# Spreading a recurrent branch over two projections, and two outputs of the next projection between a head's steps

## What is computed

```
q, k, v, o, gi, gf, xb, gate = _split(hn @ w_in, ...)      # 1024 -> 6 x 1024 and 2 x 4
h_a = sigmoid(o) * mlstm(q, k, v, gi, gf)                  # 4 heads of 256
h_a = h_a * rsqrt(mean(h_a * h_a) + EPS) * mlstm_norm
xc = causal_conv4(xb) + conv_b                             # the recurrent branch
r = sigmoid(xc @ w_r + b_r); i = sigmoid(xc @ w_i + b_i)   # 8 blocks of 128
log_a = -8 * r * softplus(-lam); a = exp(log_a)
u = sqrt(-expm1(2 * log_a)) * (i * xc)
h_b = scan(h = a * h + u) * gelu(gate)
h = h + concatenate([h_a, h_b]) @ w_out                    # 2048 -> 1024
```

## Time and profile before

| | |
|---|---|
| median of 3 runs | 2597.84 us (2596.29 to 2609.27) |
| profiled execution | 2598.1 us, its span 2596.3 us |
| mean granted PE clock | 0.972 of full speed |
| busy share of the span | PE 95%, DVE 68%, ACT 52%, POOL 0% |

### The profile page before, as it was taken

One profiled execution on the slowest core, in us unless ns is written; L12 is line 12 of the kernel. 1 busy time (PEld: TensorE's weight loads), 2 busy tenths in 40 slices (PEclk: granted clock), 3 DMA queues, 4 the chain that ended last, 5 costly groups with the idle time before them and its releaser, 6 DMA issues.

```text
span 2596.3 us, 54007 instructions
## 1 busy us (share of the span) xinstructions
PE 2457.7 (95%) x18747; PEld 2341.4 (90%) x18747; DVE 1758.2 (68%) x3497; ACT 1348.3 (52%) x2827; POOL 10.3 (0%) x17
## 2 busy tenths in 40 slices
PE   7999998979999999999999999998998999988998
PEld 7899998979989999899988999988877999877998
DVE  6566666977657677776575576656776775777764
ACT  4555556556554444465555565555663444454443
POOL 0000000000000000000000000000000000000000
PEclk9999999999999999899999999999998999998999
DMA  6535563225644333356645356643433555322553
GB/s 203 175 122 170 184 197 117 93 89 171 203 144 130 124 126 121 104 165 185 202 131 181 124 168 192 205 152 121 130 106 98 169 175 174 122 97 90 171 177 129
DMA packets 103383, 385.43 MB, mean 148 GB/s; under 512 B 11344, under 2 KB 13392, under 8 KB 103024
## 3 DMA queue, kind: packets, MB, share of 16 engines
q1 hardware_dynamic: 102784, 381.90, 46.0%
q0 software_dynamic: 496, 2.24, 0.2%
HBM read 383.05 MB, written 1.05 MB: 148 GB/s over the span
## 4 chain that ended last, share of the span: by engine, by line
PE 85%; DVE 9%; ACT 3%; issue 2%; DMA 0%; DVEq 0%; ACTq 0%; SPq 0%
PE acc L488 24%; PE acc L489 23%; PE acc L490 23%; PE acc L667 2%; DVE weights_lo L1628 2%; PE acc L651 1%; PE acc L653 1%; PE acc L652 1%; PE acc L531 1%; PE acc L746 1%; PE acc L705 1%; ACT weights_hi L1062 1%; PE acc L592 1%; PE acc L835 1%; PE acc L726 1%
## 5 line engine op out<-in xcount | busy, mean ns | idle before, releaser
L1628 DVE TENSOR_TENSOR weights_lo<-weights,weights_hi 128x512 fp32r<-128x512 f32 (+1 forms) x1392 | 905.1, 683 | 445.9 <-ACT weights_hi L1062 441.1
L488 PE MATMUL acc<-xn_parts,weights_hi 128*128 128x256 f32 (+1 forms) x3456 | 996.3, 288 | 41.4 <-DVE xn_parts L1742 14.1
L489 PE MATMUL acc<-xn_parts,weights_hi 128*128 128x256 f32 (+1 forms) x3456 | 980.3, 284 | 0.0
L490 PE MATMUL acc<-xn_parts,weights_lo 128*128 128x256 f32 (+1 forms) x3456 | 980.0, 284 | 0.0
L1062 ACT ACTIVATE weights_hi<-weights 128x512 fp32r<-128x512 f32 (+1 forms) x1392 | 811.1, 620 | 250.5 <-PE acc L490 220.6
L488 PEld LDWEIGHTS acc<-xn_parts,weights_hi 128*128 128x128 f32 x3456 | 658.3, 190 | 59.9 <-issue 46.2
L489 PEld LDWEIGHTS acc<-xn_parts,weights_hi 128*128 128x128 f32 x3456 | 657.6, 190 | 1.0
L490 PEld LDWEIGHTS acc<-xn_parts,weights_lo 128*128 128x128 f32 x3456 | 658.5, 191 | 0.0
L488 PE MATMUL acc<-arena_r,weights_hi 128*128 128x256 f32 (+1 forms) x1792 | 511.6, 285 | 9.8 <-DVE arena_r L2090 4.9
L489 PE MATMUL acc<-arena_r,weights_hi 128*128 128x256 f32 (+1 forms) x1792 | 507.3, 283 | 0.0
L490 PE MATMUL acc<-arena_r,weights_lo 128*128 128x256 f32 (+1 forms) x1792 | 507.3, 283 | 0.0
(11 more groups left out here) (286 smaller groups left out, 2494.0 us busy)
## 6 DMA issues: line engine op xcount, KB each, us to landing
weights<-in_ffn_in SPq DMA_DIRECT2D x176, 512.0 KB, 3.6
weights<-in_ffn_out SPq DMA_DIRECT2D x64, 704.0 KB, 4.1
weights<-in_att_in SPq DMA_DIRECT2D x72, 512.0 KB, 3.5
weights<-in_mlp_in SPq DMA_DIRECT2D x64, 512.0 KB, 3.4
weights<-in_mlp_out SPq DMA_DIRECT2D x64, 512.0 KB, 3.5
weights<-in_ret_qk SPq DMA_DIRECT2D x32, 512.0 KB, 3.5
weights<-in_ret_v SPq DMA_DIRECT2D x32, 512.0 KB, 3.8
weights<-in_ret_g SPq DMA_DIRECT2D x32, 512.0 KB, 3.5
```

The source lines that it names most:

```text
L488: nc.tensor.matmul(acc, hi, src_hi, start=first, stop=False)
L489: nc.tensor.matmul(acc, hi, src_lo, start=False, stop=False)
L490: return nc.tensor.matmul(acc, lo, src_hi, start=False, stop=last)
L1628: nc.vector.tensor_tensor(w_lo[sub % phase.subs][:, 0:n, :], raw[slot][:, j * SUB:j * SUB + n, :], w_hi[sub % phase.subs][:, 0:n, :].bitca ...
```

## The change

1. `mlstm_rows` is cut into three parts, done in the first units of `ab_xb`; the convolutions follow one unit each from the fourth unit of `ab_xb` to the third of `ab_gate`.
2. PE computes the two gate products of chunk m right behind unit m of `ab_gate`, in banks 4 to 7. ACT does the sigmoids, a Square and a Tanh there, and the gelu's Tanh one unit later.
3. In the first head's units ACT does the exponent of a chunk per unit, and logarithm and exponent over half the branch (1088 columns) in place of DVE's reciprocals. Square root, products, scans, output and its split are DVE and ACT operations over 2176 columns (scans over 272) in the turns of the heads before the last.
4. The sigmoid of o is one operation of 544 columns per head behind the head's last unit; the fifth turn goes.
5. The last head's steps stand between the pieces of outputs 0 and 1 of `ab_out` (`part_output`): the branch's tiles first, then those of heads 0 and 1, of head 2, and of head 3. `branch_first` reorders the weight rows for it; size and number of the loads stay. `ab_out` then begins with its third output.

The diff, cut to what the mixer's steps need:

```diff
+                tiles = ((8, 9, 10, 11), (12, 13, 14, 15), (0, 1, 2, 3), (4, 5), (6, 7))
+                def part_output(sub, o, part):
+                    pe.wait_ge(split_ready, after.sub0 + sub + 1)
+                    for k in tiles[part]:
+                        pe.wait_ge(*((A["mixed"], k // 2 + 1) if k < DC else (lru_sem["done"], 1)))
+                        last = product(PS[:, o, 0:S2], w_hi[sub % after.subs][:, k % SUB, :], w_lo[sub % after.subs][:, k % SUB, :],
+                                       (ab_hi[k], ab_lo[k]), k == 8, k == 7)
+                    if part != 3:
+                        last.then_inc(sub_multiplied, 1)
...
+                            pe.wait_ge(lru_sem["gates_ready"], 2 * DC)
...
+                last_head = A_HEADS - 1
+                scores(last_head)
+                turn_v(last_head)
+                pe.wait_ge(out_evacuated, evacuated(phase))
+                part_output(0, 0, 0)
+                mix(last_head)
+                part_output(1, 0, 1)
+                part_output(2, 1, 0)
+                part_output(3, 1, 1)
+                part_output(4, 0, 2)
+                head_sum(last_head)
+                part_output(5, 1, 2)
+                part_output(6, 0, 3)
+                part_output(7, 1, 3)
+                part_output(6, 0, 4)
+                part_output(7, 1, 4)
...
+            def gate_projection(src):
+                phase, L = ph["ab_gate"], lru_sem
                 pe.wait_ge(consts2_loaded, 48)
+                for m in range(phase.units):
+                    pe.wait_ge(out_evacuated, FREE_BANKS + phase.out0 - SLOTS + 1 + m)
+                    multiply(phase, m // phase.body, m % phase.body, PS[:, m % SLOTS, 0:S2], src)
+                    pe.wait_ge(L["conv_ready"], m + 1)
+                    if m >= 2:
+                        pe.wait_ge(L["gates_ready"], 2 * (m - 1))
+                    else:
+                        pe.wait_ge(ab_sem["log_in"], 1)
                     for gate, w in ((0, w_r), (1, w_i)):
+                        last = nc.tensor.matmul(PS[:, 4 + 2 * (m % 2) + gate, 0:S2], w[:, m, :], lru_xc[:, m, :], start=True, stop=True)
                     last.then_inc(L["gates_summed"], 1)
...
+                    dense_outputs(ph["ab_out"], lambda k: (ab_hi[k], ab_lo[k]), S2, lambda k: (ab_sem["mixed"], A_HEADS), 1)
...
+            def gelu(c):
+                act.wait_ge(lru_sem["gelu_in"], c + 1)
+                nc.scalar.activation(gelu_t[:, c, :], sq[:, c % 4, :], ACT.Tanh, scale=math.sqrt(2.0 / math.pi))\
+                    .then_inc(lru_sem["gelu_ready"], 1)
+            def gate_projection():
+                L, phase = lru_sem, ph["ab_gate"]
+                nc.scalar.preload_act_table(ACT.Sigmoid)
+                for m in range(phase.units):
...
+                    wait_unit(phase, m // phase.body, m % phase.body)
+                    nc.scalar.activation(lru_gate[:, m, :], PS[:, m % SLOTS, 0:S2], ACT.Copy).then_inc(out_evacuated, 1)
+                    act.wait_ge(L["gates_summed"], m + 1)
+                    for gate, dst, bias in ((0, lru_a, "lru_b_r"), (1, lru_i, "lru_b_i")):
+                        nc.scalar.activation(dst[:, m, :], PS[:, 4 + 2 * (m % 2) + gate, 0:S2], ACT.Sigmoid, bias=param(bias, m))\
+                            .then_inc(L["gates_ready"], 1)
+                    act.wait_ge(out_evacuated, evacuated(phase, m + 1))
+                    nc.scalar.activation(sq[:, m % 4, :], lru_gate[:, m, :], ACT.Square, scale=math.sqrt(0.044715))\
+                        .then_inc(L["gelu_squared"], 1)
+                    act.wait_ge(L["gates_ready"], 2 * m + 1)
+                    nc.scalar.activation(lru_r[:, m, :], lru_a[:, m, :], ACT.Tanh, scale=lam8_neg[:, m:m + 1]).then_inc(L["tanh_ready"], 1)
+                    if m:
+                        gelu(m - 1)
...
+                def output_gate(hd):
+                    o = proj2[:, 24 + 2 * hd:26 + 2 * hd, :]
+                    nc.scalar.preload_act_table(ACT.Sigmoid)
+                    act.wait_ge(out_evacuated, evacuated(phase, (hd + 1) * phase.body))
+                    nc.scalar.activation(o, o, ACT.Sigmoid).then_inc(A["o_ready"], 1)
+                def decay(c):
+                    nc.scalar.activation(lru_a[:, c, :], lru_a[:, c, :], ACT.Exp, scale=lam8[:, c:c + 1]).then_inc(L["decay_ready"], 1)
+                def logarithm(n):
+                    act.wait_ge(L["tanh_ready"], DC)
+                    act.wait_ge(L["input_ready"], DC)
+                    part = slice(n * half, (n + 1) * half)
+                    nc.scalar.activation(y[:, part, :], lru_r[:, part, :], ACT.Ln, bias=one).then_inc(L["logged"], 1)
+                def inverse(n):
+                    act.wait_ge(L["logged"], n + 1)
+                    part = slice(n * half, (n + 1) * half)
+                    nc.scalar.activation(y[:, part, :], y[:, part, :], ACT.Exp, scale=-1.0).then_inc(L["inverse_ready"], 1)
+                def root():
+                    act.wait_ge(L["root_in"], 1)
+                    nc.scalar.activation(lru_r[:, :, :], lru_r[:, :, :], ACT.Sqrt, scale=2.0).then_inc(L["root_ready"], 1)
...
+                        if n == 0:
+                            if i == 0:
+                                gelu(DC - 1)
+                            if i == 1:
+                                root()
+                            exp_tables()
...
+                            decay(n)
+                            if 1 <= n <= 2:
+                                logarithm(n - 1)
+                            if 3 <= n <= 4:
+                                inverse(n - 3)
+                        wait_unit(phase, i, n)
+                        nc.scalar.activation(proj2[:, 8 * (n // 2) + 2 * i + n % 2, :], PS[:, n % 2, 0:S2], ACT.Copy)\
+                            .then_inc(out_evacuated, 1)
+                        if n == 7:
+                            output_gate(i)
...
+                after, hd = phase.after, A_HEADS - 1
+                exp_tables()
+                split(after, 0, 1)
+                weights(hd)
+                values(hd)
+                split_part(after, 0, 2, 0)
+                denominator(hd)
+                split_part(after, 0, 2, 1)
+                squares(hd)
+                split(after, 0, 3)
+                factor(hd)
...
+            def lru_input(c):
+                L = lru_sem
+                dve.wait_ge(L["gates_ready"], 2 * c + 2)
+                nc.vector.tensor_tensor(lru_i[:, c, :], lru_i[:, c, :], lru_xc[:, c, :], ALU.mult).then_inc(L["input_ready"], 1)
+                dve.wait_ge(L["gelu_squared"], c + 1)
+                stt(sq[:, c % 4, :], sq[:, c % 4, :], 1.0, lru_gate[:, c, :], ALU.add, ALU.mult).then_inc(L["gelu_in"], 1)
+            def gate_projection():
+                phase = ph["ab_gate"]
+                for m in range(phase.units):
...
+                    if m < 3:
+                        lru_conv(m + 5)
+                    if m:
+                        lru_input(m - 1)
...
+                        if i == 0:
+                            if n == 0:
+                                lru_input(DC - 1)
+                            if n == 2:
+                                lru_gelu()
...
+                            if n == 7:
+                                lru_root_in()
...
+                        if i == 1:
+                            if n == 3:
+                                lru_forced()
+                            if n >= 6:
+                                lru_scan(n - 6)
+                        if i == 2:
+                            if n == 3:
+                                lru_out()
+                            if n == 6:
+                                lru_rounded()
+                            if n == 7:
+                                lru_rest()
+                after, hd = phase.after, A_HEADS - 1
+                take(hd - 1)
+                split(after, 0, 1)
+                shifts(hd)
+                weights(hd)
+                split_part(after, 0, 2, 0)
+                denominator(hd)
+                split_part(after, 0, 2, 1)
+                gated(hd)
+                split(after, 0, 3)
+                take(hd)
...
+    def branch_first(u):
+        heads = u[[0, 2]].reshape(2, P, 2, 4 * P)
+        return np.concatenate([u[[1, 3]], np.stack([heads[:, :, n].transpose(1, 0, 2).reshape(P, 8 * P) for n in range(2)]), u[4:]])
```

More of the change, by code:

```diff
@@ L1024, in _ @@
                     dense_outputs(ph["ab_xb"], src, S2, ready)
[L1025 to L1029, removed]
+                    gate_projection(src)
+                    mlstm(src)
+                    dense_outputs(ph["ab_out"], lambda k: (ab_hi[k], ab_lo[k]), S2, lambda k: (ab_sem["mixed"], A_HEADS), 1)
                 else:
@@ L1155, in turn @@
                             unit(i - 1, phase.body - 1)
-                turn(0, True)
+                if ahead:
+                    split(phase, 1, 0)
```

(40 more changed lines are left out.)

267 lines of the change are left out of this document (117 added, 150 removed).

## The result

The changed kernel took 2573.03 us (median of 4 runs, 2562.95 to 2579.35) against 2597.61 before, a ratio of 0.9894 with a 95% interval of 0.9855 to 0.9934.

The account below looks back on a forecast made before the run. PE was taken to bound the kernel, except in two stretches where it waits for ACT and DVE. 2598.1 − 7.6 (between the projections) − 21.1 (tail) + 4 (clock) = 2573.4 us, forecast 2573, range 2564 to 2583.

Parts of the forecast that it names:

- The stretch between the projections: Between the projections, 20.2 us before: 12.6 us were to remain, so 7.6 us less.
- Products: Gate products on PE in `ab_gate`: 1.05 us per chunk, 8.4 us for 8 chunks, if PE stays busy.
- Ring in `ab_gate`: Units 1 and 2: the loop split, convolution, input, gelu takes 5.0 us against PE's 4.09, twice, costing about 0.8.
- Start of `ab_qkvo`: ACT's queue makes unit 2's piece late, 0.4 + 2.05, and DVE's gelu product adds 0.4: 2.9 us.
- Root in the second head's turn: Two table loads and the root are covered by `scores`, except about 0.5 us at unit 2.
- The tail's schedule: From the end of the heads' units, U: 84.3 us before, 63.2 after at full clock, so 21.1 us less.
- The clock: PE's clock falls behind the 2.4 us wait among fp32 products in the last head; cost taken as 4 us.
- the sign of being wrong: The prediction is wrong if PE's clock stays at half through the pieces of outputs 0 and 1.
- the ring in `ab_gate`: Rival: engines there wait for each other, nothing overlapping, 8.6 us per unit against 4.09; 2611 us, chance 3 in 100.
- time given back in the turns: Rival: splits queue behind wide DVE operations and table loads, eight exposing about 1.1 us each; 2581 us, chance 14.
- a table switch cost more than its load: Rival: five bare switches of ACT's function table each take the load's 1.28 us again; 2579 us, chance 2.
- the clock stays up: Rival: the 2.4 us wait passes without a fall of PE's clock; 2569 us, chance 25 in 100.

Follow-up runs that it names:

- e6: The changed kernel with both the edits of e3 and of e5; 2558.24 us (median of 6 runs).
- e1: The changed kernel with the last head's steps together again and `ab_out` whole behind them, the branch still spread; 2590.32 us, single execution.
- e4: The changed kernel with 18 useless matmuls on PE where it would wait ahead of `mix`; 2559.45 us, single execution.
- The repeated kernel: The changed kernel unaltered, timed again on the chip of e6; 2567.34 us (median of 5 runs).
- e2: The changed kernel with gate products, sigmoids and DVE's input behind `ab_gate` instead of in its units; 2571.23 us, single execution.
- e5: The changed kernel with the first head's last gelu, table load, exponents, logarithms and inverses one unit later, DVE's gelu product two; 2582.74 us, single execution.
- e3: The changed kernel with the last head's shifts, exponents, weights and values ahead of the splits and the sigmoid of o; 2555.79 us, single execution.
- e7: The changed kernel with all four pieces over the branch's tiles ahead of `mix`; 2568.23 us, single execution.

## Why the prediction was right

The time was forecast as 2573 and came out at 2573.03. That closeness has luck in it, as its terms show.

- **The stretch between the projections**: 7.6 us less were forecast for the first part, 7.4 measured. Products: 8.4 forecast as 1.05 per chunk, 7.3 measured (8 × 0.91), since I priced them by their shown length and not from start to start. Ring in `ab_gate`: 0.8 forecast, one wait of 0.8 (L1450) and small stalls of 0.5, 1.3 in all. Its own numbers give 1.2: 5.0 against 4.09 twice is 1.8 late, less the 0.6 to spare. Start of `ab_qkvo`: 2.9 forecast as 0.4, 2.05 and 0.4; the waits were 0.3 and 1.86, and matched instruction by instruction with e6, which has only the first, the changed kernel without a fall (e1, e4) loses 2.4 us there. Root in the second head's turn: 0.5 forecast, no wait in the trace. Not forecast: in this execution the clock fell behind the 1.86 us wait, which cost 1.2 (200.3 against 199.1 in e1 and e4). The sum came near because these errors cancel.
- **The tail's schedule**: the wait ahead of `mix` 2.4 forecast, 2.4 measured; none above 1 us ahead of `head_sum`, as forecast; the tail with the clock up 63.2 forecast, 63.7 in e4, whose only difference is that PE does not idle.
- **The clock**: the step that was off, by its size. "I take 4, nearer the upper end" was 6.3 (70.0 against 63.7), of it 4.3 in `mix` (10.3 against 6.0) and 2.1 in the four pieces (8.25 against 6.1). The clock stood at half for 13.65 us, not "under 10". The repeated kernel had 10.24 us of it and paid 4.7 (68.4 − 63.7). The bounds of 0 to 8.1 held both. It was back up 4.4 us into the pieces (1930.66 + 13.65 = 1944.31), so the sign of being wrong, half clock all through them, was not met.
- **The sum against the time**: the stretch that the change touches lost 21.7 us (292.0 − 270.3), 3 less than the 24.7 forecast, and 23.1 in the repeat. The profiled pair lies 29.4 us apart by the spans (2596.3 and 2566.9), because PE reached the mixer 9.5 us earlier (1720.84, and 1730.38 in the earlier trace rows), in a part of the program that the change doesn't touch; behind the mixer 1.8 were lost again, whose cause I did not look for. The interval of the ratio, 17 to 38 us, cannot tell 21.7 from 24.7.
- **The rivals**: the ring in `ab_gate` (2611) and time given back in the turns (eight times 1.1 us, which is 8.8 and not the 8 of its sum) were not seen; between the start of `ab_qkvo` and U no wait of PE above 0.3 us stands apart from those named. Nor did a table switch cost more than its load: in the last head's chain the load at 1923.63 starts 0.01 us behind the sigmoid, takes 1.28 us, and the rounding behind it starts at 1924.92, 0.01 us after its end. The Trainium skill, page "ScalarE: Activation LUTs", section "What ACT_TABLE_LOAD costs", adds a drain; the trace doesn't show one here, and the measurement decides. That the clock stays up had 25 in 100; behind the wait ahead of `mix` it fell in all four traces that have it (changed, e2, e5, repeat).

## What to carry to other kernels

Of the 14.3 us that the tail lost, 11.5 came with work taken off the last turn of the pipeline and 2.8 with work put between its steps; look first for what need not be there at all. The second figure is what is left after the fall of the clock: with the lists reordered so that PE doesn't wait (e3), the tail is 8.7 us shorter still. When a wait of PE is priced, count what the clock loses behind it: a wait of 2.4 us ahead of fp32 matmuls cost 6.3 more, while one of 4.1 us (e7) was followed by only 3.4 us at half. Two engines' lists reordered (e3) or even useless matmuls in the gap (e4) took the 6.3 back. With a scatter of up to 20 us between executions of one kernel, compare marks inside the traces, from one event to another around the change.

## What the runs showed of the hardware

**A short wait brings the clock down in some executions and not in others, and not with equal odds.** In the ten traces the wait of 2.8 us ahead of the norm's sum (the first in the earlier trace rows) was followed by a fall in nine, the one of 2.84 ahead of the gates in four, the one of 1.86 at the start of `ab_qkvo` in one of seven, and the one of 2.4 ahead of `mix` in four of four. In e1 one of 1.5 ahead of `mix` was enough. The first two are about equally long. What differs is what PE did before: dense work with the one, 6 us of fp32 sums with waits around them with the other; which property decides was not tried. Each fall at the gates cost between 1.2 and 2.7 us (gates to the 100th matmul behind, against e6). In `mix`, which is fp32, the fall lasted longest; behind the pieces' dense matmuls it ended.

**The same matmuls at the same granted clock go at two paces.** One window of the first block, in code that is equal in all kernels, of before and then of the changed kernel:

```profile
260.00:400.00 140.00, 139.97 (x1189) 139.77 (x1188) 88.26 (x162) 75.64 (x149) 0.00 (x0) 1.00 0.60 191
```

```profile
260.00:400.00 140.00, 139.73 (x1233) 139.53 (x1232) 90.81 (x166) 78.19 (x153) 0.00 (x0) 1.00 0.62 196
```

PE is busy throughout and the clock is 1.00 in both, but 1233 matmuls of 256 columns fit in one and 1189 in the other: 0.1135 and 0.1177 us each. Either pace holds for a stretch of a layer, and which one comes where differs from execution to execution, of one kernel too (ahead of the mixer some 2300 starts at the slower pace in the changed kernel's first trace, 1900 in its second). Matmuls 1600 to 3200 took 209.4 us before (251.3 to 460.6) and 201.5 in the changed kernel (250.4 to 451.9). The pace is the greater part of what moves PE's arrival at the mixer between 1716.60 and 1740.62: ahead of the mixer some 5800 starts in e1 and 870 in e3 follow the one before at the slower pace, and 4930 × 0.0042 is 20.7 of these 24.0 us. Matmuls of 272 columns went at 0.1266 in every trace. The cause stays open.
